# A fourth projection of the first head joins the chunk-by-chunk opening of an encoder-layer kernel

## What is computed

```python
mod = jax.nn.silu(c) @ ada_w[l] + ada_b[l]
sh1, sc1, g1, sh2, sc2, g2 = jnp.split(mod, 6, axis=-1)
h = _modulate(_rmsnorm(x, mix_pre_w[l]), sh1, sc1)     # rmsnorm(x) * (1 + sc1) + sh1
proj = h @ w_in                                         # 2048 x (7 x 8 heads x 128)
rq, rk, rv, rg, dq, dk, dv = jnp.split(proj, points, axis=-1)
```

## Time and profile before

| what | value |
|---|---|
| median of three runs | 3246.96 us |
| the profiled execution: its own time | 3248.8 us |
| the profiled execution: span | 3247.0 us |
| PE busy in the span | 3145.6 us (97%) |
| DVE busy | 2751.7 us (85%) |
| ACT busy | 1081.1 us (33%) |
| POOL busy | 956.7 us (29%) |
| mean granted TensorE clock | 0.992 |
| chain that ended last, by engine | PE 80%, DVE 7%, POOL 5%, DMA 5% |

### The profile page before, as it was taken

One profiled execution on the slowest core, in us unless ns is written; L12 is line 12 of the kernel. 1 busy time (PEld: TensorE's weight loads), 2 busy tenths in 40 slices (PEclk: granted clock), 3 DMA queues, 4 the chain that ended last, 5 costly groups with the idle time before them and its releaser, 6 DMA issues.

```text
span 3247.0 us, 48996 instructions
## 1 busy us (share of the span) xinstructions
PE 3145.6 (97%) x19669; PEld 2985.9 (92%) x19669; DVE 2751.7 (85%) x3943; ACT 1081.1 (33%) x1401; POOL 956.7 (29%) x562
## 2 busy tenths in 40 slices
PE   7999999998999988999999999998999999999998
PEld 3788888888997878999999999998999999999998
DVE  4688888888888999969888888887788889888888
ACT  2222332323224235942323332332323332332333
POOL 2100000002545895022323333233223334333332
PEclk9999999999999999999999999999999999999999
DMA  9845444445546313789999999998799999999997
GB/s 392 312 168 173 167 165 169 163 173 195 207 174 251 128 45 110 226 281 380 368 372 382 367 372 365 375 375 319 298 373 374 365 369 364 374 368 368 361 360 297
DMA packets 175242, 929.09 MB, mean 286 GB/s; under 512 B 16919, under 2 KB 50636, under 8 KB 79948
## 3 DMA queue, kind: packets, MB, share of 16 engines
q1 hardware_dynamic: 123790, 553.15, 46.2%
q0 software_dynamic: 51264, 373.32, 29.6%
HBM read 891.11 MB, written 33.69 MB: 285 GB/s over the span
## 4 chain that ended last, share of the span: by engine, by line
PE 80%; DVE 7%; POOL 5%; DMA 5%; issue 1%; SPq 1%; ACT 1%; DVEq 0%; POOLq 0%; ACTq 0%
PE ps_all L1179 18%; PE ps_all L1242 9%; PE ps_all L1248 9%; PE ps_all L1186 9%; PE ps_all L1243 9%; PE ps_all L831 8%; PE ps_all L833 7%; PE ps_all L832 7%; DMA sb_small<-in_ada_w 2%; DMA sb_raw_ring<-in_v_t 1%; DVE sb_hot L2314 1%; POOL sb_route_b L2554 1%; DVE sb_hot L2311 1%; POOL sb_route_b L2551 1%; POOL sb_route_b L2552 1%
## 5 line engine op out<-in xcount | busy, mean ns | idle before, releaser
L1621 ACT ACTIVATE sb_raw_hi<-sb_raw_ring 128x2048 fp32r<-128x2048 f32 x256 | 490.9, 1918 | 1135.2 <-DMA sb_raw_ring<-in_v_t 552.0
L2222 DVE TENSOR_TENSOR sb_raw_lo<-sb_raw_ring,sb_raw_hi 128x2048 fp32r<-128x2048 f32 x256 | 585.4, 2287 | 74.3 <-ACT sb_raw_hi L1621 73.9
L1242 PE MATMUL ps_all<-sb_w_hi,sb_raw_hi 128*128 128x336 f32 x2032 | 625.6, 317 | 21.2 <-ACT sb_raw_hi L1621 15.2
L1179 PE MATMUL ps_all<-sb_h_lo,sb_raw_hi 128*128 128x336 f32 x2048 | 636.6, 318 | 0.0
L1179 PE MATMUL ps_all<-sb_h_hi,sb_raw_hi 128*128 128x336 f32 x2016 | 627.0, 318 | 0.0
L1243 PE MATMUL ps_all<-sb_w_lo,sb_raw_hi 128*128 128x336 f32 x2032 | 624.6, 316 | 0.0
L2571 POOL DMA_INDIRECT sb_gather_ring<-in_u_tab,sb_kept x178 | 282.2, 1585 | 756.0 <-DVE sb_kept L2363 586.6
L2571 POOL DMA_INDIRECT sb_gather_ring<-in_v_tab,sb_kept x178 | 306.9, 1724 | 599.5 <-DVE sb_acc_a L2376 385.5
L1242 PEld LDWEIGHTS ps_all<-sb_w_hi,sb_raw_hi 128*128 128x128 f32 x2032 | 383.9, 189 | 23.9 <-ACT sb_raw_hi L1621 16.3
L1179 PEld LDWEIGHTS ps_all<-sb_h_lo,sb_raw_hi 128*128 128x128 f32 x2048 | 386.1, 189 | 0.0
L1243 PEld LDWEIGHTS ps_all<-sb_w_lo,sb_raw_hi 128*128 128x128 f32 x2032 | 383.6, 189 | 0.0
(11 more groups left out here) (343 smaller groups left out, 5556.2 us busy)
## 6 DMA issues: line engine op xcount, KB each, us to landing
sb_raw_ring<-in_u_t SPq DMA_DIRECT2D x128, 1024.0 KB
sb_raw_ring<-in_v_t SPq DMA_DIRECT2D x128, 1024.0 KB
sb_arena<-in_ada_wt SPq DMA_DIRECT2D x94, 512.0 KB, 6.0
sb_w_raw<-in_w_t SPq DMA_DIRECT2D x32, 1024.0 KB, 4.9
sb_small<-in_ada_w SPq DMA_DIRECT2D x30, 1024.0 KB, 11.5
sb_w_raw<-in_w_v SPq DMA_DIRECT2D x32, 768.0 KB, 4.3
sb_g_ring<-table_scratch SPq DMA_DIRECT2D x32, 672.0 KB
table_scratch<-sb_stage SPq DMA_DIRECT2D x7, 2688.0 KB, 12.3
```

Source lines behind the costliest of these rows:

```text
L1179: last = mm(acc, raw_hi[:, r[0], kk * P:(kk + 1) * P], part, start=i == 0, stop=False)
L1242: mm(accs[c], v, w_hi[:, slots[e], :], start=e == 0, stop=False)
L1621: acti(raw_hi[:, k % 2, :], raw_ring[:, k % RAW, :], ACT.Copy).then_inc(S["un_hi"], 1)
L2222: vec.tensor_tensor(raw_lo[:, k % RAW, :], raw_ring[:, k % RAW, :], raw_hi[:, k % 2, :].bitcast(f32), ALU.subtract)\
```

## The change

The weights of projection 3 are loaded after piece 12 and split at block 3. From piece 13 on, the `ada_w` pieces of slots 3 and 4 go to the room of x. The products of projection 3 join the order from piece 19, with up to three products in a piece from there on, all due before piece 31. Its sum stands in bank 6. `project(0, 3)` is gone: 48 of 64 products stand in the pieces, 16 after the last. The first value piece (piece 4) is loaded right after the last `ada_w` piece, and DVE does low 4 ahead of late piece 0, low 5 ahead of late piece 1. POOL takes the whole of the fourth remainder, and the DVE half with its waits (PE's and SP's on `h_odd`) goes.

```diff
-ADA_FULL = 25
+ADA_MOVED = 13
+LAST_USES = 30
...
-W_READY = (7, 8, 11)
+W_READY = (7, 8, 11, 19)
...
-        slots.append([queue.pop(0)[3:] for _ in range(2) if queue and queue[0][0] <= p])
+        slots.append([queue.pop(0)[3:] for _ in range(2 if p < W_READY[3] else 3) if queue and queue[0][0] <= p and p < ADA_PIECES - 1])
...
         def ada_place(n):
-            return ada_late[n - ADA_FULL - 3] if n in (ADA_FULL + 3, ADA_FULL + 4) else ada_ring[ada_slot(n)]
+            return ada_late[ada_slot(n) - 3] if n >= ADA_MOVED and ada_slot(n) >= 3 else ada_ring[ada_slot(n)]
+
+        def first_bank(n):
+            return bank(n if n < 3 else 6)
...
-                if n == ADA_FULL + 3:
+                if n == ADA_MOVED:
                     sp.wait_ge(S["xtr"], KD)
...
                 wait(sp, "w_low", 8 * h + n - 1)
-                if isinstance(h, int) and h == 0 and n == 5:
-                    sp.wait_ge(S["h_odd"], BLOCKS + 1)
...
                 if n == 8:
                     piece_load(0, 2)
+                if n == 12:
+                    piece_load(0, 3)
...
-            piece_load(0, 3)
+            piece_load(0, 4)
             sp.wait_ge(S["silu_out"], 16)
 
-            sp.wait_ge(S["ada_done"], ADA_FULL + 5)
+            sp.wait_ge(S["ada_done"], LAST_USES)
...
             sp.wait_ge(S["ada_done"], ADA_PIECES)
             col_load(0, 0)
-            piece_load(0, 4)
             col_load(0, 1)
...
-                last = split_products(bank(n), ((high, low), (h_hi[:, k, :], h_lo[:, k, :])), k == 1, k == KD - 2)
+                last = split_products(first_bank(n), ((high, low), (h_hi[:, k, :], h_lo[:, k, :])), k == 1, k == KD - 2)
...
-            for n, k in ((1, KD - 3), (2, KD - 3), (0, KD - 4), (1, KD - 4), (2, KD - 4)):
+            for n, k in [(n, KD - 3) for n in range(1, 4)] + [(n, KD - 4) for n in range(4)]:
                 chunk_product(n, k)
-            for n in range(3):
+            for n in range(4):
                 chunk_product(n, KD - 1)
                 chunk_product(n, KD - 2)
...
-                    if h is not None and not (a is None and n < 3):
+                    if h is not None and not (a is None and n < 4):
                         project(h, n)
...
                     if n == 3:
-                        act.wait_ge(S["ada_done"], ADA_FULL)
+                        act.wait_ge(S["ada_done"], ADA_MOVED - 3)
...
+                if j == 3:
+                    split_high(0, 3)
...
-            split_high(0, 3)
             head_step(0, None)
...
-            dve.wait_ge(S["w_high"], 4)
-            vec.tensor_tensor(w_fourth[:, 1, WT // 2:], w_raw[:, 1, WT // 2:], w_fourth[:, 0, WT // 2:].bitcast(f32), ALU.subtract)\
-                .then_inc(S["h_odd"], 1)
-
...
                 if a is None:
+                    low(4)
                     late(0)
-                    low(4)
-                    late(1)
                     low(5)
-                    late(2, 3, 4)
+                    late(1, 2, 3, 4)
                     low(6)
...
-            first_low(3)
+                if j == 3:
+                    first_low(3)
```

More of the change, by code:

```diff
@@ L457, in ada_slot @@
         def ada_slot(n):
-            return n % ADA_RING if n < ADA_FULL else (0, 1, 2, 3, 4, 0, 1)[n - ADA_FULL]
+            return n % ADA_RING
         def ada_use(n):
@@ L839, in chunk_product @@
                 c = slice(k * P, (k + 1) * P)
-                high, low = (w_third[:, 0, c], w_third[:, 1, c]) if n == 2 else (w_high[:, n, c], w_low[:, n, c])
-                last = split_products(bank(n), ((high, low), (h_hi[:, k, :], h_lo[:, k, :])), k == 1, k == KD - 2)
+                place = own_place(0, n)
+                high, low = (place[:, 0, c], place[:, 1, c]) if place is not None else (w_high[:, n, c], w_low[:, n, c])
+                last = split_products(first_bank(n), ((high, low), (h_hi[:, k, :], h_lo[:, k, :])), k == 1, k == KD - 2)
                 if k == KD - 2:
@@ L872, in project @@
                 r = n % 2
[L873 to L876, removed]
+                high, low = w_high[:, r, :], w_low[:, r, :]
                 if n < 4:
@@ L1416, in evacuate @@
                     dst = (k_t, q_t, dk_t, dq_t)[n]
-                    acti(dst, bank(n), ACT.Copy, scale=P ** -0.5 if n == 0 else 1.0).then_inc(S["proj_ev"], 1)
+                    acti(dst, first_bank(n) if isinstance(h, int) and h == 0 else bank(n), ACT.Copy, scale=P ** -0.5 if n == 0 else 1.0).then_inc(S["proj_ev"], 1)
                 else:
@@ L2466, in first_low @@
                 high, low = (place[:, 0], place[:, 1]) if place is not None else (w_high[:, n], w_low[:, n])
-                w = WT // 2 if n == 3 else WT
-                nc.gpsimd.tensor_tensor(low[:, 0:w], w_raw[:, n % 2, 0:w], high[:, 0:w].bitcast(f32), ALU.subtract)\
+                nc.gpsimd.tensor_tensor(low, w_raw[:, n % 2, :], high.bitcast(f32), ALU.subtract)\
                     .then_inc(S["w_low"], 1)
```

## The result

| | before | after |
|---|---|---|
| median of 22 runs each | 3249.47 us | 3256.18 us |
| lowest to highest | 3238.17 to 3260.34 | 3249.24 to 3263.54 |
| profiled execution, own time | 3248.8 | 3257.75 |
| its span | 3247.0 | 3255.9 |

The ratio is 1.0027, 95% interval 1.0018 to 1.0037, which is 6 to 12 us. It isn't the quotient of the two medians, which lie 6.7 us apart (1.0021); that is inside the interval too. So the times do show a loss. The predicted time and range hold, but "no difference by the times" doesn't: 22 runs on either side resolve 0.1%, not the 0.3% that I allowed.

The account below looks back on a forecast made before the run. PE was taken to bound the kernel, with transfers also full in the opening. Head 1 later by 1.6 (opening and products) + 2.65 + 1.85 - 0.3 = 5.9 us took 3246.96 to 3252.9 us; range 3245 to 3258.

Parts of the forecast that it names:

- no difference by the times: Whole kernel: a slowdown of 0.18% is below the 0.3% (9.7 us) that a measurement can tell; chance 0.92.
- Part 2: Opening, fourth weights' 1.05 MB ahead of piece 13: costs 0 to 2.5 us, taken as 2.5, piece 18 at 76.8 us.
- PE can't win time back in the loop: Loop from head 0 on: PE has no idle time, so a later start of head 1 moves the end as much.
- Part 1: Opening, `ada_w` pieces 19 to 28: 12 products move in at 0.70 us each, 8.4 us more PE ahead of piece 31.
- x: End of the products: the moment ACT begins to evacuate projection 2, forecast at 128.7 us, before at 117.43.
- Part 4: Ahead of the first value block: cover by `project(0, 3)` gone, PE waits 2.65 us for ACT's split 4, DVE's low 4.
- Part 5: Head 0: DVE starts its late pieces later and delays PE's last blocks, +1.85 us; head 1 at x + 39.3.
- Rival A: Opening: stays bound by its transfers, 12 products fit, piece 31 at 109.1, head 1 at 160.7, 3245.6 us; chance 0.18.
- Rival B: First value block: clock falls at the new wait, costing 1.75 or 5.1 us, 3254.7 or 3258.0 us; chance 0.12.
- Rival C: Opening and head 0: the transfer is hidden and DVE's chain has more room, 3247 to 3249 us; chance 0.10.
- The number: Start of head 1 and whole kernel: head 1 at 168.0 in place of 162.12, +5.9 us, giving 3252.9 us.

Follow-up runs that it names:

- change_again: The changed kernel run once more with nothing altered; ratio 1.0024 to the kernel before.
- change_third: The changed kernel run a third time with nothing altered, one execution only; its own time 3248.85 us.
- early_transfer: The changed kernel with the fourth weights transferred behind piece 10 instead of 12 and projection 3's products from piece 16; ratio 1.0016 to the kernel before.
- late_first: The changed kernel with DVE's order of before: late piece 0, low 4, late piece 1, low 5; ratio 1.0021 to the kernel before.
- products_back: The changed kernel with projection 3's 16 products back behind the pieces, its weight transfer left in the middle; ratio 1.0025 to the kernel before.
- best_of_both: Changed kernel with weights behind piece 10, products from piece 16, split 4 early, value piece 5 fetched behind piece 4, one late piece behind low 8; ratio 1.0000.

## Why the prediction was right in its mechanism, and what failed

The mechanism held nearly everywhere, and two steps of the prediction failed. The one that made the forecast wrong is the resolution: "about 0.3% (9.7 us) is what a measurement of this kernel can tell from no change", a figure for which the prediction gives no row. By it a forecast of +5.9 us (0.18%) was called "no difference by the times" with 0.92. The runs showed that 22 runs on either side tell 0.1%, and the ratio was 1.0027 [1.0018, 1.0037]: a loss. The other is a term of the sum that was too small: Part 2, the transfer at 2.5 us and at the full clock, where piece 20 started 0.2, 2.2 and 3.6 us later than forecast. The parts, one by one:

- **PE can't win time back in the loop**: right. From head 1 to the stream it was 1020.0 to 1022.5 us in the ten profiles with a changed opening, whatever head 1's delay.
- **Part 1**: right in its prices of full pieces: 20 to 23 started 3.27 us apart (3.3). The products gain where they fill a wait, and that was more than I had. From the start of piece 19 to the end of the fourth projection it was 51.46 us before and 49.21 in the change (79.58 to 128.79, where the wait of 2.59 begins): 2.25 us less, of which 1.39 are the wait ahead of piece 31. Timeline of PE before, piece 19:
```profile
76.88 1.06 PE L810 MATMUL ps_all<-sb_small,sb_arena 128*32 128x512 f32 x8
```
  So from piece 20 to x I had 45.0 us and it was 43.6, a term 1.4 too large. About 0.7 of it is pieces 29 and 30, which I priced at 1.20 each: that row held some 0.3 us in which PE wasn't paced by its own work, and in the change, with the transfers ahead of PE, they took 0.88 and 0.86. About 0.5 is the way from piece 31 to x, 11.8 us where I had 12.3.
- **Part 2**: the term that was mis-sized. I took 2.5 us as the upper bound of the cost, with piece 18 at 76.8. The transfer itself made the pieces 2.4 us later, as priced; but the stretch of small loads behind piece 16 was up to 0.9 us longer than before's 5.3 to 5.6, and the waits on pieces 17 and 18 came to 3.66 us, with piece 18 at 77.65. And I priced it at the full clock: behind these waits the clock fell in two of the three profiles of the change, for 1.55 and 2.8 us more. Piece 20 was to start at 83.7; it started at 83.86, 85.86 and 87.29. Its mean is 2.0 later than forecast, which outweighs the 1.4 above. That the number of head 1 came out is thus in part luck: two errors of 2.0 and 1.4 with opposite signs. Why the stretch behind piece 16 varies wasn't settled.
- **Part 4**: right to 0.1 us: 2.59 for 2.65 in three profiles, and the edit of ACT's order alone removed it.
- **Part 5**: right: x + 39.3, and v to head 1 35.4 for 33.8; the edit of DVE's order alone removed it. In change_again, without a low clock at the value block, PE waited 0.23 us ahead of the last value block and 1.28 ahead of head 1, where I had 0.35 and 1.5. Low 9 held nothing up.
- **Rival A**: wrong. Piece 31 started at 115.6 to 119.1, not 109. The busy share of PE's weight loads went from 13.93 to 16.65 of 32 us only, and yet PE was full. By the rule that the Trainium skill gives (Perfetto Trace Analysis, section Identifying the Most-Contended Engine), which judges TensorE by the share of the peak rate that it reaches and by the busy share of LDWEIGHTS, the second of these left room. The trace doesn't agree: here the distance between starts told the room, and no engine's busy share did.
- **Rival B**: the mechanism is real, at another place than I put it. Behind the value block's wait the clock fell in the first profile, in change_third and in early_transfer, not in change_again and late_first. Where it fell, the first value block took 9.9 to 10.0 us for 8.45. But it cost nothing at head 1, since DVE's chain was as late as PE anyway (x + 39.3 at either clock). It cost something at the waits that I had placed in the sum at full clock.
- **Rival C**: wrong: neither the transfer nor DVE's chain stayed hidden.
- **The number**: head 1 was to be at 168.0, and was at 168.6 in the mean of three. My base was the median of 3 runs, 3246.96; the median of 22 is 3249.47. So of the 3.3 us by which 3256.18 exceeds 3252.9, 2.5 are the base.
- **Open**: products_back gave 1.0025, at least 4.5 us, where its head 1 was 1.7 us late. Its repetition gave 1.0012. And in all nine ratios of kernels with a changed opening the ratio says more than head 1 does, by 1 to 6 us, some 2 in the mean, while each single ratio is uncertain by 3 to 5 us. Either the executions that weren't profiled had the longer waits and the low clock, or something beyond head 1 costs 2 us in the changed kernels: from head 1 to the stream the four profiles of the kernel before and its copies took 1021.9, 1017.6, 1021.3 and 1017.0 us, 1.6 less in the mean than the ten. The stream from there took 2065.9 in the mean of the ten and 2063.1 in the mean of the four, with single values from 2055.9 to 2071.9. Four such values don't settle it.

## What to carry to other kernels

Moving a transfer into a stretch where transfers are full costs its whole length at the consumer, unless other work of that consumer stands ready at the piece where it shows; here it took the transfer two pieces earlier and with it products for the piece where the delay lands, and even so 0.7 to 1.1 us of wait stayed at another piece. When work that stood between two dependent steps is moved away, list what it covered on each engine (ACT's split, DVE's low part, a load behind a long queue), and reorder all of these in the same edit: mending one alone moved the wait to the next. And judge a change of 5 us in 3250 by marks that don't scatter (the start of the next stage, the same to 0.1 us given the mark before), then by many runs.

## What the hardware showed that was not expected

- The same program took two ways through the opening: 3.6 us of waits on two pieces, or 0.50 us where PE was already 2.7 us late from an earlier low clock. In late_first PE was 4.2 us late there and had none. A slower PE hid a transfer.
- Behind waits of 3.0 to 3.7 us on two successive pieces the clock went to its lower level for 3.4 and 6.8 us in two of four profiles, and stayed up in the others; behind a single wait of 2.5 to 2.6 us, for 3.4 us in three of five.
- A 768 KB load queued behind two broadcasts of 1 MB each landed 10.7 us after its issue, where the median of its kind is 4.3 us over the run. Being ahead of the broadcasts didn't shorten it: in best_of_both, issued among the last pieces, it took 10.9 us (103.67 to 114.55). Its earlier issue is what helped.
- Three small loads between two pieces of 1 MB, 200 KB together, made the distance of the two landings 5.0 to 6.2 us in the fourteen profiles, where it is 2.5 for pieces that follow each other.
